# Norm sums and roots tracked one by one, first weights behind x blocks, last conv tile in the h buffer, last output block in halves

## The reference

```
x = x + 0.5 * SwiGLU_1(RMSNorm(x))                       # 1024 -> 2*2816 -> 1024
h = RMSNorm(x)
conv_glu | q | k | v | gates = h @ W_in                   # 2048 + 1024 + 256 + 256 + 2*1024 columns
a = (silu(layernorm(causal_conv31(u * sigmoid(g))))) @ W_proj
b = (sliding-window attention, 16 query heads, 4 kv heads, window 128, bias, sinks) @ W_o
x = x + (sigmoid(g_a) * a + sigmoid(g_b) * b) @ W_out
x = x + 0.5 * SwiGLU_2(RMSNorm(x))
```

## Time and profile before

| | us |
|---|---|
| runs | 3040.81, 3515.44, 3035.76 |
| median of the runs | 3040.81 |
| profiled execution | 3036.41 |
| its span, slowest core (core 7) | 3034.8 |
| spans of the eight cores | 3018.6 to 3034.8 |
| granted TensorE clock, mean | 0.996 to 0.998 of 2.4 GHz |
| PE busy | 2973.1 (98% of the span) |
| POOL, ACT, DVE busy | 743.4, 836.3, 1236.7 |

### The profile page before, as it was taken

The page is one execution under the profiler, slowest core; times in us unless marked ns, Lnnn a source line. Parts: engine busy times, 40 slices in busy tenths (PEclk is TensorE's granted clock), DMA queues, the critical chain, the costliest instruction groups (busy, mean ns, idle before and its releaser), DMA issues.

```text
span 3034.8 us, 41593 instructions; the slowest of 8 cores (3018.6 to 3034.8 us)
## 1 busy us (share of the span) xinstructions
PE 2973.1 (98%) x14660; PEld 1340.0 (44%) x14660; DVE 1236.7 (41%) x1700; ACT 836.3 (28%) x1482; POOL 743.4 (24%) x655
## 2 busy tenths in 40 slices
PE   6999999999999999999899999999999999999998
PEld 3444444444444454454334434434444444444443
DVE  4323345423344223757444454553323333223333
ACT  4111123211123222414666656642211111111110
POOL 3100012100003434293465555563000000000000
PEclk9999999999999999999999999999999999999999
DMA  7514249513148677967934545689442139332102
GB/s 181 92 23 70 35 115 239 105 21 60 21 100 218 133 181 174 221 121 231 179 81 138 143 140 149 161 194 237 138 90 42 21 69 228 87 63 35 18 1 111
DMA packets 330440, 354.09 MB, mean 117 GB/s; under 512 B 228352, under 2 KB 230400, under 8 KB 330240
## 3 DMA queue, kind: packets, MB, share of 16 engines
q1 hardware_dynamic: 295104, 252.82, 29.7%
q0 software_dynamic: 35136, 98.62, 20.4%
HBM read 294.79 MB, written 117.44 MB: 136 GB/s over the span
## 4 chain that ended last, share of the span: by engine, by line
PE 91%; DMA 3%; DVE 2%; SPq 1%; issue 1%; ACT 1%; POOL 1%; DVEq 0%; ACTq 0%; POOLq 0%
PE ps L480 91%; DMA zsh<-z_s 1%; SPq L513 1%; DMA z_s<-zfm 1%; DVE bst L828 1%; DMA sg<-sig_s 1%; DVE y L836 0%; DMA x<-x 0%; DVE y L838 0%; SPq L516 0%; ACT rs L501 0%; DMA hA<-xn 0%; POOL pt L959 0%; ACT tfM L501 0%; ACT et L501 0%
## 5 line engine op out<-in xcount | busy, mean ns | idle before, releaser
L480 PE MATMUL ps<-hA,wup 128*128 128x512 bf16 x5632 | 1226.7, 379 | 1.4 <-DVE sg L999 0.7
L480 PEld LDWEIGHTS ps<-hA,wup 128*128 128x128 bf16 x5632 | 551.1, 98 | 667.0 <-issue 5.7
L480 PE MATMUL ps<-wdn,hid 128*128 128x512 bf16 x2768 | 605.0, 379 | 0.0
L501 ACT ACTIVATE tfA<-ps 128x512 f32<-128x512 f32 x352 | 209.8, 597 | 1432.9 <-PE ps L480 1430.6
L644 DVE TENSOR_TENSOR hid<-ps,tfA 128x512 bf16<-128x512 f32 x346 | 238.9, 691 | 878.2 <-PE ps L480 867.4
L658 DVE SCALAR_TENSOR_TENSOR x<-ps,x 128x512 f32<-128x512 f32 x512 | 351.4, 690 | 228.9 <-PE ps L480 228.6
L480 PEld LDWEIGHTS ps<-wdn,hid 128*128 128x128 bf16 x2768 | 270.7, 98 | 326.7 <-issue 0.3
L959 POOL TENSOR_TENSOR pt<-et,EB 128x1024 bf16<-128x1024 bf16 x126 | 270.2, 2167 | 136.4 <-ACT et L501 135.0
L480 PE MATMUL ps<-hB,wG 128*128 128x512 bf16 x1024 | 229.2, 379 | 0.0
L480 PE MATMUL ps<-hB,wS 128*128 128x512 bf16 x1024 | 224.0, 379 | 0.0
L501 ACT ACTIVATE tfB<-ps 128x512 f32<-128x512 f32 x192 | 112.0, 595 | 318.8 <-PE ps L480 267.0
(11 more groups left out here) (79 smaller groups left out, 1817.1 us busy)
## 6 DMA issues: line engine op xcount, KB each, us to landing
x<-x SPq DMA_DIRECT2D x96, 512.0 KB, 7.8
sig_s<-tfB SPq DMA_DIRECT2D x128, 256.0 KB, 5.0
sg<-sig_s SPq DMA_DIRECT2D x128, 256.0 KB, 3.6
wup<-w1u POOLq DMA_DIRECT2D x44, 512.0 KB, 6.8
wup<-w2u POOLq DMA_DIRECT2D x44, 512.0 KB, 7.4
xM<-x SPq DMA_DIRECT2D x32, 512.0 KB, 5.6
x<-xM SPq DMA_DIRECT2D x32, 512.0 KB, 5.0
out<-x SPq DMA_DIRECT2D x32, 512.0 KB, 3.6
```

The costliest lines, as they stand in the source:

```text
L480: inst = e.matmul(o, l, r, start=st, stop=sp)
L501: return e.activation(**kw)
```

## The change

Seven things change. (1) The planner's bandwidth for SP goes from 0.25e6 to 0.38e6 bytes per us and that for POOL from 0.25e6 to 0.24e6. (2) The sums, means and roots of the norms get one token for each column instead of the granule that four share. (3) At the start the first weight slice waits for the first x block, the second for the fourth, and the other four for the DVE instruction of the fourth norm; x8 to x11 wait for the third slice, x12 to x15 for the fifth. (4) `cact` gets a second buffer at 88 KB, for the last tile alone; its load is added right behind that of the tile before. (5) Stage C takes its h buffers in another order, and the one at 88 KB last. (6) In stage C the weights of the second quarter wait for the last `up` of the first tile instead of its first. (7) The last block of the output is stored in two halves, each behind its own DVE instruction.

```diff
-DMA_GBPS = 0.25e6
+DMA_GBPS = {"sp": 0.38e6, "pool": 0.24e6}
...
-                server[e] = max(t0 + both + (o.nbytes - both * DMA_BOTH) / DMA_GBPS, free[e])
-                server[other] += both * (1.0 - DMA_BOTH / DMA_GBPS)
+                server[e] = max(t0 + both + (o.nbytes - both * DMA_BOTH) / DMA_GBPS[e], free[e])
+                server[other] += both * (1.0 - DMA_BOTH / DMA_GBPS[other])
...
-    cact = buf("cact", 56, [KC, T], BF16)
+    cacts = [buf("cact%d" % i, [56, 88][i], [KC, T], BF16) for i in range(2)]
...
-        act(junk.v(), xblk.v(), AF.Square, D, accum=s_.v(c))
+        sv, mv, rv = [View(lambda a=b.t[:, c]: a, [(name, k)]) for name, b in (("ss", s_), ("ms", m_), ("rstd", r_))]
+        act(junk.v(), xblk.v(), AF.Square, D, accum=sv)
...
-        hs = hA if first_norm else [hA[1], hA[2], hA[3], hA[0]]
+        hs = hA if first_norm else [hA[3], hA[1], hA[0], hA[2]]
...
+                if xn_dst is None and (s, i, tb) == (1, 3, 3):
+                    for hf in range(2):
+                        c = slice(512 * hf, 512 * hf + 512)
+                        dma("sp", "x%d" % (12 + hf), x_dst[r0:r0 + 128, c], xt.t[:, c], [xt.v(c)], [(dst_tok, r0 // 128, hf)], 128 * D * 2)
+                    continue
...
             got = load_x(0, 0)
-            w = [load_up(f0)]
-            for f in range(f0 + 1, f1):
-                w.append(load_up(f, got[-1:]))
+            w = [load_up(f0, got[:1]), load_up(f0 + 1, got[3:4])]
             load_x(0, 1)
-            load_x(0, 2, w[1:2])
-            got = load_x(0, 3, w[3:4])
+            make_h_pe(0)
+            for f in range(f0 + 2, f1):
+                w.append(load_up(f, [normed[0]]))
+            load_x(0, 2, w[2:3])
+            got = load_x(0, 3, w[4:5])
             for f in range(f0, f1):
                 load_dn(f, got[-1:])
-            done = set()
+            done = {0}
...
                     if s == 0 and q == 0:
                         load_x(0, i, [last[0]])
-                        if i == 0:
-                            hold = [last[0]]
                     up(i, f0 + 1, f1, hd, 1)
+                    if s == 0 and q == 0 and i == 0:
+                        hold = [last[0]]
...
-        o = ob[t % 2]
+        o, cact = ob[t % 2], cacts[t == NT - 1]
...
-        if t > 1:
+        if 1 < t < NT:
             load_cact(t - 1)
+        if t == NT - 1:
+            load_cact(t)
```

More of the change, by code:

```diff
@@ L547, in norm_block @@
         c = slice(k % 4, k % 4 + 1)
-        act(junk.v(), xblk.v(), AF.Square, D, accum=s_.v(c))
+        sv, mv, rv = [View(lambda a=b.t[:, c]: a, [(name, k)]) for name, b in (("ss", s_), ("ms", m_), ("rstd", r_))]
+        act(junk.v(), xblk.v(), AF.Square, D, accum=sv)
         if use_pool:
             pool(lambda e: e.tensor_scalar(out=m_.t[:, c], in0=s_.t[:, c], scalar1=1.0 / D, scalar2=EPS,
-                                           op0=ALU.mult, op1=ALU.add), [s_.v(c)], [m_.v(c)], 0.3)
+                                           op0=ALU.mult, op1=ALU.add), [sv], [mv], 0.3)
             pool(lambda e: e.tensor_tensor(out=r_.t[:, c], in0=m_.t[:, c], in1=mh.t[:, 0:1], op=ALU.pow),
-                 [m_.v(c), mh.v()], [r_.v(c)], 0.72)
+                 [mv, mh.v()], [rv], 0.72)
         else:
-            act(m_.v(c), s_.v(c), AF.Ln, 1, bias=EPS, scale=1.0 / D)
-            act(r_.v(c), m_.v(c), AF.Exp, 1, scale=-0.5)
-        dve(lambda e: e.scalar_tensor_tensor(out=xn_out.t[:], in0=xblk.t[:], scalar=r_.t[:, c], in1=gain.t[:],
+            act(mv, sv, AF.Ln, 1, bias=EPS, scale=1.0 / D)
+            act(rv, mv, AF.Exp, 1, scale=-0.5)
+        return dve(lambda e: e.scalar_tensor_tensor(out=xn_out.t[:], in0=xblk.t[:], scalar=r_.t[:, c], in1=gain.t[:],
                                              op0=ALU.mult, op1=ALU.mult),
-            [xblk.v(), r_.v(c), gain.v()], [xn_out.v()], D)
+            [xblk.v(), rv, gain.v()], [xn_out.v()], D)
     def load_tr(key, dst, src, row0, rtok, after=(), tag=""):
@@ L595, in make_h @@
                 load_tr("hA%d" % i, hs[i], xn_src, r0, [("xn3", r0 // 128 + tb) for tb in range(4)])
+        normed = [None]
         def make_h_pe(i):
@@ L600, in make_h_pe @@
                 xn = xnAr.next()
-                norm_block(xb[4 * i + tb], gA, xn, junkA, True)
+                normed[0] = norm_block(xb[4 * i + tb], gA, xn, junkA, True)
                 for q in range(2):
@@ L1035, in load_cact @@
     def load_cact(t):
-        load_tr("cact", cact, cact_d, t * T, [("cact", t // 4, r) for r in range(16)], tag="cact")
+        load_tr("cact%d" % (t == NT - 1), cacts[t == NT - 1], cact_d, t * T, [("cact", t // 4, r) for r in range(16)], tag="cact")
     for j in range(2):
```

## The result

| | before | after |
|---|---|---|
| executions, median, us | 3035.76 | 3066.57 |
| ratio to before | | 1.0097, interval 1.0074 to 1.0119 |
| profiled execution, us | 3036.41 | 3067.58 |

The forecast was 3040, with a range from 3026 to 3052.

The account below looks back on a forecast made before the run. PE, busy 98% of the span, was taken as the bound, leaving only its gaps, clock and ends. Start -2.7, stage B +8.7, end of M -2.0, last block -0.5 gave +3.5 on 3036.4: 3040 us, range 3026 to 3052.

Parts of the forecast that it names:

- a gap in a place that has none now: Any place in the kernel: one of the listed signs that would show the forecast wrong; no size given.
- Stage B, +8.7: Stage B: faster planned SP puts the conv before one glu unit, so PE waits longer for its input; +8.7 us.
- 5.2 + 3.5: Stage B's first half: three already waiting groups wait 1.72 us more each (5.2), the other five 0.7 each (3.5).
- The rival given 0.10: Stage B: the conv's waits take PE's clock down in several of eight groups; 3054 us if all, chance 0.10.
- End of stage M, -2.0: End of stage M: one cact load goes, gates issue sooner, PE's 2.02 us wait for them ends; -2.0 us.
- +6.2: End of stage M, upper end: the four sg loads come to stand behind one more transposed load; +6.2 us.
- the rival given 0.18: End of stage M clears: POOL's weight stands elsewhere, 8.4 us goes with the clock; 3032 us, chance 0.18.
- Start, -2.7: Start: four weight issues move behind the fourth norm, so its root runs at 20.41 instead of 23.11; -2.7 us.
- the 4.76: Start: time from the fourth norm's root to the first up matmul, taken to stay unchanged at 4.76 us.
- Last block, -0.5: End of output: the last half-block of 256 KB lands in 2.2 us where 512 KB take 2.7; -0.5 us.
- The 2%: Whole kernel: about what a measurement can tell from none, 61 us, more than all terms together.

Follow-up runs that it names:

- e_Aold: Kernel after, with stage A's DMAs alone planned at the old bandwidths: 3060.75 us, ratio 1.0074 to the kernel before.
- e_xlate: Kernel after, with the planner taking x loads of stage A's second half to land 16 us later: profiled execution 3052.15 us.
- a_oldmc: Kernel after, with the old single cact buffer, h buffer order and weight release in stage C: 3069.71 us, ratio 1.0103 to the kernel before.
- e_sgl: Kernel after, with the planner taking the last tile's gate (sg) loads to land 6 us later: 3060.71 us, ratio 1.0083 to the kernel before.
- a_oldtok: Kernel after, with the norms' old shared tokens: ratio 1.0110 to the kernel before.
- b_tok: Kernel before, with the norms' separate tokens alone added: ratio 1.0009 to the kernel before.
- a_oldrate: Kernel after, with the planner's old bandwidths (0.25e6 for both queues): 3036.24 us, ratio 0.9996 to the kernel before.
- v_slow: Kernel before plus new start order, separate tokens and output halves, with both planned bandwidths at 0.21e6 throughout: profiled execution 3047.96 us.
- v_Bslow: Kernel before plus new start order, separate tokens and output halves, with stage B alone planned at 0.21e6: ratio 1.0008 to the kernel before.

## Why the prediction was wrong

**The step that failed: the planner's bandwidth, costed in stage B alone.** The forecast was +3.5; the profiled execution became 31.2 longer. The constant acts on every SP transfer. For stage A the prediction argued from PE's waits of before ("later in stages A and M PE has no wait for xnA ... elsewhere they are worth nothing"), which was said of the tokens, and the bandwidth was not carried through A at all. There it cost 11.3 us on the median core and 12.0 on the slowest, as it planned Squares ahead of their x blocks and of silus that PE was to wait for (e_Aold and e_xlate both bring 455.8 back). The rows of before could have shown it: no wait of PE, but ACT waiting 1.84 for an x block in that stretch, with nothing urgent behind. The prediction's own sign of being wrong, "a gap in a place that has none now", is what came.

**Stage B, +8.7.** The sign and the mechanism were right: the conv stands directly behind 64 gate matmuls. On the slowest core it was +13.8, on the median core +4.6; over the five kernels with this order the median core has +2.1 to +9.0, so that the 8.7 is no better confirmed than that. The sizes were not: four of eight groups waited, not nearly all, and the first group, counted as covered by one unit, was covered by six and waited 3.86 where 4.78 was put in. PE's waits for zsh were 10.8 us in all, 9.9 of them in the first half (the three shown and one of 1.09), where 5.2 + 3.5 more than 4.1 (12.8) had been forecast; the loads were quicker, with a median of 4.5 from 1015 to 1200 where 5.3 was put in the earlier trace rows. The clock came on top: 5.63 + 3.18 + 3.18 us of PE's work at half speed, 6.0 us. The waits' growth, 5.8, and this make 11.8 of the 13.8; the rest was not placed. The rival given 0.10 was half right, at three groups of eight. The Trainium skill (TensorE: Matmul & The Clock Gate, Part 1: The HAM clock gate) says that an idle engine falls to half its clock and that activity brings it back; the trace agrees with it here, at waits of 2.27, 2.66 and 3.86 us, where the prediction saw it borne out for the longest wait only (the 3.06 of core 7 before was followed by no fall). The second half, left at nothing, gave +2.3, and +4.8 on the slowest core (its wait of 4.81 for y); what caused that was not tested.

**End of stage M, -2.0.** Measured +7.1 at the change-over and +1.8 before it. The upper end of this term, +6.2, named what happened: "if the four sg loads come to stand behind one more transposed load". The row has it, 7.53 us. The middle was taken from the cact load that goes; the step overlooked that a faster planned SP moves the gates' use forward as well. With it the merge moved ahead of the up matmuls that had stood in front of the last projection (24 left of 112). That POOL's wait for the hA load would stay was right (8.78 us, 12.01 before), but not what was to follow from it: from 1990 to 2090 PE's longest wait for POOL's pt is 1.7 on core 4, where it had been 3.3 with the half clock behind it, so the rival given 0.18 came true at its place. PE's wait of 2.02 did go too, and the change-over was longer all the same. With these bandwidths the new buffers are not the reason (a_oldmc), the planned landing of the gates is (e_sgl).

**Start, -2.7.** Measured -3.4, near by two errors that cancel. The issues did move behind the fourth root, and on core 4 it runs at 15.90, 7.2 sooner than on core 7 before. But the 4.76 from it to the first up matmul did not stay: they became 7.55, since PE has the fifth block's transposes in front, as before, and that block's Square now waited 3.18 for its x block. On the slowest core 3.3 of the 4.4 won are given back in the first quarter (PE's wait of 2.60 at 46.47, with half the clock for 3.4 us behind it), on the median core nothing. And the prediction gave the gain to the order and nothing to the tokens; the order without the tokens gives nothing (a_oldtok, 27.0), the tokens without the order 2.5 (b_tok), both with the old bandwidths 4.9 (a_oldrate, 26.7 to 21.8).

**Last block, -0.5.** 2.1 us for 256 KB, against 2.6 for 512 KB in the same execution, and 0.4 less from the last matmul to the end: right. By the rule of the Trainium skill that the prediction gives beside this term it would have been 2.6 and 3.2; the page has it for DMAs that GpSimd issues, and these are SP's.

**The sum.** The medians of the stages add up to -3.4 + 11.3 + 4.6 + 2.3 + 1.8 + 7.1 = +23.7, the slowest core's to +31.6 (+31.2 with the 0.4 won behind the last matmul). Waits for transfers fall unevenly over the cores, and the time is that of the worst. The prediction summed one core's rows as if it stayed the slowest; it was core 7 before and core 4 after. The 2% that it took for what a measurement can tell from none is too much: the intervals here reach 0.1 to 0.4% to either side.

## What to carry to other kernels

A constant in a planner's model is a change to every order that the planner writes: go through all stages for instructions that wait for a transfer, whether or not the busiest engine waits for them now, and ask what will stand behind each on its own engine if it is planned earlier. A landing believed too early takes away the work that covered it, and it can stop more than its own consumer, since an engine in order holds back whatever is ready behind it; a landing believed too late is no remedy for everything either (v_slow, v_Bslow). To find which belief costs, move the planned landing of one kind of transfer and leave the chip's work as it is.

## What the runs showed of the hardware

On core 4 of the kernel after, each of the nine stretches at half clock between the first up matmul and the last followed a gap of 2.3 to 5.8 us on PE and lasted 3.4 or 6.8 us; on core 7 of the kernel before a gap of 3.06 was followed by none. In stage B's first half this added 6.0 us to waits of 9.9. A transposed load of 1 MB held SP's queue for 5.4 to 7.5 us at the change-over (3.8 to 8.8 over both kernels; see the earlier trace rows), so that loads of 256 KB behind it are late by that much. And the landing of an x block took 12 to 14 us in the median where stage A's halves meet, against 2.6 for a store of the same 512 KB at the end.
